# Two of eight column blocks of a gated norm on POOL instead of DVE, in a two-block transformer kernel

## The reference

```
rmsnorm(u, g) = u * rsqrt(mean(u * u) + EPS) * g

xl_new = xl + ml[2] * rmsnorm(y_l, g_post_mix[i])        # the gated norm
h2     = modulate(rmsnorm(xl_new, g_pre_mlp[i]), ml[3], ml[4])
xl_new = xl_new + ml[5] * rmsnorm(sqrelu_mlp_2(h2, ...), g_post_mlp[i])
# and the same for the context xc, with mc instead of ml, where the layer isn't the last
```

## Time and profile before

| | |
|---|---|
| median of 3 runs | 1733.2 us (1731.16 to 1733.64) |
| the profiled execution | 1732.92 us |
| its span | 1731.1 us |
| PE busy | 1624.5 us (94%) |
| DVE busy | 1155.1 us (67%) |
| ACT busy | 541.2 us (31%) |
| POOL busy | 342.6 us (20%) |

### The profile page before, as it was taken

How to read it: one execution, slowest core, us unless ns; L and a number is a source line. 1 busy time by engine, 2 the same in 40 slices (tenths; PEclk the granted TensorE clock), 3 DMA queues, 4 the chain that set the end, 5 groups by cost and what they waited for, 6 DMA issues and landing times.

```text
span 1731.1 us, 26810 instructions
## 1 busy us (share of the span) xinstructions
PE 1624.5 (94%) x10898; PEld 1420.1 (82%) x10898; DVE 1155.1 (67%) x1668; ACT 541.2 (31%) x1106; POOL 342.6 (20%) x308
## 2 busy tenths in 40 slices
PE   7998989999899999999888899999999988879997
PEld 6887789998788999988546588888888875679997
DVE  6754877777877788869764574444444778577776
ACT  4434241112333122153575440101012455641112
POOL 1100323332222333300000111111111100023331
PEclk9999999999999999999999999999999989989999
DMA  7843755556655555443101323222222241125551
GB/s 297 283 177 138 255 197 184 187 186 220 229 181 200 182 185 186 170 175 98 61 1 37 134 73 99 96 98 97 97 97 87 73 134 37 63 95 184 184 185 56
DMA packets 69939, 247.53 MB, mean 143 GB/s; under 512 B 7504, under 2 KB 10576, under 8 KB 69712
## 3 DMA queue, kind: packets, MB, share of 16 engines
q1 hardware_dynamic: 69840, 246.18, 41.7%
HBM read 245.10 MB, written 1.05 MB: 142 GB/s over the span
## 4 chain that ended last, share of the span: by engine, by line
PE 73%; DVE 14%; issue 7%; ACT 5%; DMA 1%; POOL 0%; SPq 0%; DVEq 0%; ACTq 0%; POOLq 0%
PE psum L371 20%; PE psum L373 19%; PE psum L372 19%; DVE lo_ring L334 2%; PE psum L1112 2%; PE psum L386 1%; PE psum L387 1%; PE psum L388 1%; DVE c_soft L2125 1%; ACT c_p L1914 1%; DVE r_x L1525 1%; DVE c_conf L2021 1%; DVE c_p L2133 1%; PE psum L486 1%; PE psum L1743 1%
## 5 line engine op out<-in xcount | busy, mean ns | idle before, releaser
L2289 POOL TENSOR_SCALAR hi_ring<-raw_ring 128x1024 fp32r<-128x1024 f32 x304 | 342.4, 1128 | 1366.9 <-PE psum L373 967.3
L334 DVE TENSOR_TENSOR lo_ring<-raw_ring,hi_ring 128x1024 fp32r<-128x1024 f32 x348 | 499.8, 1437 | 60.0 <-POOL hi_ring L2289 23.0
L371 PE MATMUL psum<-x_hi,hi_ring 128*128 128x256 f32 (+1 forms) x1464 | 465.0, 318 | 30.1 <-DVE lo_ring L334 13.6
L372 PE MATMUL psum<-x_lo,hi_ring 128*128 128x256 f32 (+1 forms) x1464 | 459.8, 314 | 0.0
L373 PE MATMUL psum<-x_hi,lo_ring 128*128 128x256 f32 (+1 forms) x1464 | 459.5, 314 | 0.0
L371 PEld LDWEIGHTS psum<-x_hi,hi_ring 128*128 128x128 f32 x1464 | 284.7, 194 | 53.8 <-issue 22.4
L371 PE MATMUL psum<-hid_hi,hi_ring 128*128 128x256 f32 (+1 forms) x992 | 303.3, 306 | 0.0
L373 PE MATMUL psum<-hid_hi,lo_ring 128*128 128x256 f32 (+1 forms) x992 | 302.1, 305 | 0.0
L372 PE MATMUL psum<-hid_lo,hi_ring 128*128 128x256 f32 (+1 forms) x992 | 301.2, 304 | 0.0
L372 PEld LDWEIGHTS psum<-x_lo,hi_ring 128*128 128x128 f32 x1464 | 284.8, 195 | 15.1 <-issue 0.2
L373 PEld LDWEIGHTS psum<-x_hi,lo_ring 128*128 128x128 f32 x1464 | 284.7, 194 | 15.1
(11 more groups left out here) (423 smaller groups left out, 1997.7 us busy)
## 6 DMA issues: line engine op xcount, KB each, us to landing
raw_ring<-weights SPq DMA_DIRECT2D x460, 512.0 KB, 3.3
h_const<-hyb_consts SPq DMA_DIRECT2D x1, 1088.0 KB, 11.6
x<-xT SPq DMA_DIRECT2D x1, 1024.0 KB, 5.8
x<-ctxT SPq DMA_DIRECT2D x1, 1024.0 KB, 17.0
outT<-x SPq DMA_DIRECT2D x4, 256.0 KB, 2.5
shared<-shared_consts SPq DMA_DIRECT2D x1, 398.0 KB, 13.7
par<-params SPq DMA_DIRECT2D x1, 301.5 KB, 6.4
```

Source lines behind the costliest of these rows:

```text
L334: nc.vector.tensor_tensor(lo_ring[:, s, :], raw_ring[:, UNIT_AT[u] % RAW_SLOTS, :], hi_ring[:, s, :].bitcast(F32), ALU.subtract).then_inc( ...
L371: nc.tensor.matmul(bank(u % BANKS, T), w_hi, hi[:, k, 0:T], start=(k == 0), stop=False)
L372: nc.tensor.matmul(bank(u % BANKS, T), w_hi, lo[:, k, 0:T], start=False, stop=False)
L2289: nc.gpsimd.tensor_scalar(hi_ring[:, n % SPLIT_SLOTS, :], raw_ring[:, slot, :], 1.0, 0.0, ALU.mult, ALU.add).then_inc(hi_ready, 1)
```

## The change

In layer 0's gated norm POOL takes blocks 3 and 7, product and addition, and DVE the other six. POOL's product goes to relu2 instead of normed. POOL counts a flag of its own, pool_updated, and ACT waits for this one ahead of the squares of blocks 3 and 7. DVE's additions of blocks 4 and 6 (the order of the places being 0, 1, 2, 4, 5, 6) must keep the count that ACT's other waits look for, so block 4 counts 2 (for 3 and 4) and block 6 counts 2 (for 6 and 7). POOL's piece stands ahead of its split of the MLP's unit 4, the one that waits for PE to finish the MLP's unit 0. Layer 1 isn't changed, nor are PE and SP.

```diff
     def squares_act(act, n, T, src, name, at, place=None):
         for k in range(KT):
-            act.wait_ge(flag(name), at + k + 1)
+            if T == TB and k in POOL_BLOCKS:
+                act.wait_ge(flag("pool_updated"), POOL_BLOCKS.index(k) + 1)
+            else:
+                act.wait_ge(flag(name), at + k + 1)
             nc.scalar.activation(sq[:, k, 0:T], src[:, k, 0:T], ACT.Square).then_inc(flag("norm_sq"), 1)
...
-        for c, (a, b) in enumerate(GATED[T]):
+        for c, (a, b) in enumerate([p for p in GATED[T] if T == SEQ or p[0] not in POOL_BLOCKS]):
             t = normed_chunk(c, a, b, T)
             by = rstd[:, 0:T].unsqueeze(1).broadcast_to([P, b - a, T])
             link(nc.vector.tensor_tensor(t, y[:, a:b, 0:T], by, ALU.mult))
-            nc.vector.tensor_tensor(x[:, a:b, 0:T], t, x[:, a:b, 0:T], ALU.add).then_inc(flag("x_updated"), b - a)
+            counts = COUNTED[a] if T == TB else b - a
+            nc.vector.tensor_tensor(x[:, a:b, 0:T], t, x[:, a:b, 0:T], ALU.add).then_inc(flag("x_updated"), counts)
+
+    POOL_BLOCKS = (3, 7)
+    COUNTED = {0: 1, 1: 1, 2: 1, 4: 2, 5: 1, 6: 2}
+
+    def gated_pool(pool, n):
+
+        pool.wait_ge(flag("norm_rstd"), n + 1)
+        pool.wait_ge(flag("y_scaled"), KT * ((n - 3) // 2))
+        for i, k in enumerate(POOL_BLOCKS):
+            nc.gpsimd.tensor_tensor(relu2[:, i, :], y[:, k, :], rstd[:, :], ALU.mult).then_inc(flag("pool_product"), 1)
+            pool.wait_ge(flag("pool_product"), i + 1)
+            nc.gpsimd.tensor_tensor(x[:, k, :], relu2[:, i, :], x[:, k, :], ALU.add).then_inc(flag("pool_updated"), 1)
...
             for n, u in enumerate(SPLIT_UNITS):
+                if u == U_L2MLP[0] + 4:
+                    gated_pool(pool, LAYERS[0].norm + 1)
                 if u in ACT_HI:
                     continue
```

## The result

| | before | changed |
|---|---|---|
| median of 20 runs | 1732.59 us | 1738.07 us |
| ratio | | 1.0025, 95% interval 1.0017 to 1.0032 |
| the profiled execution, its span | 1732.92, 1731.1 us | 1737.69, 1735.8 us |

The changed kernel is slower by 0.25%, 4.3 us (2.9 to 5.5); this is the distance of the means, 1737.49 and 1733.20 us, while the medians are 5.5 us apart. Two later measurements of the same code gave 1.0015 and 1.0027; all three together are about 3.9 us.

The account below looks back on a forecast made before the run. The prediction took PE waiting for DVE in layer 0's gated norm as the bound. Turns +3.12, two pairs gone -2.65 and a second tail block +0.86 gave +1.3 us on 1733.2, so 1734.5 us, range 1731.1 to 1737.9.

Parts of the forecast that it names:

- Where the kernel is bound, and that it passes on: In layer 0's gated norm PE waits for DVE; what the norm gains or loses passes one for one to the end.
- Two pairs away, -2.65: Two of DVE's eight product and addition pairs leave its chain in the gated norm, 2.65 us less.
- Turns between DVE and POOL: In the gated norm DVE operations with both inputs in SBUF alternate with POOL's four operations, +3.12 us; chance 0.57.
- rival A: DVE and POOL work side by side in the norm without hindering each other, -1.79 us, 1731.4 us; chance 0.10.
- The price of a turn: Each POOL operation between two of DVE's in the norm costs DVE 0.78 us, four of them +3.12 us.
- p: Time of one new POOL operation in the norm, taken as 1.05 us, with ends of 0.53 and 2.1 us.
- The second block in the tail, +0.86: After DVE's end PE has two blocks to add instead of one before the statistics, +0.86 us.
- Rival D, the clock: PE falls to half clock in the norm's sums, +1.7 us on top, +3.0 in all, 1736.2 us; chance 0.11.
- Rival B: POOL's two-input operations in the norm take well above 1.05 us, giving 1738.7 us at 2.1 us each; chance 0.10.
- C: POOL comes late in the norm, after DVE's queued operations or by a slow first start, 1734.9 or 1733.8 us; chance 0.12.
- C's second case: POOL's first product in the norm starts 6 us late, at 982.9; claimed +0.6 us, 1733.8 us.
- POOL's flags hold nobody: POOL finishes blocks 3 and 7 at 979.9 and 982.8, before ACT reaches them at about 984 and 988.

Follow-up runs that it names:

- e3: The changed kernel with rstd and the products for DVE in PSUM, so each DVE operation has one SBUF input; ratio 0.9985 to the kernel before.
- e2: The changed kernel without POOL's four operations, blocks 3 and 7 of the update left out; ratio 0.9988 to the kernel before.
- e4: The changed kernel with rstd and the products for DVE in PSUM and POOL on blocks 2 and 5; ratio 0.9980 to the kernel before.
- e8: The changed kernel itself, measured a second time with nothing altered; ratio 1.0015 to the kernel before.
- e6: The changed kernel with only block 3 on POOL and seven blocks on DVE; ratio 1.0003 to the kernel before.

## Why the prediction was right in its mechanism and small in its size

- **Where the kernel is bound, and that it passes on**: right. M rose by 2.82 us and PE's first MLP matmul moved from 17.32 to 20.13 us after the first product, +2.81; behind the MLP it was +2.95 (332.06 to 335.01 us). That this goes one for one to the end the traces can't show: the part behind the MLP takes 419.4 to 425.0 us, whichever the kernel.
- **Two pairs away, -2.65**: right but for 0.14 us, the two additions that count by 2 and start 0.07 us late. That edit I had costed at nothing.
- **Turns between DVE and POOL**: right, against rival A. e3 shows the condition.
- **The price of a turn**: the term that was mis-sized. I took p = 1.05 from the operation with one input of 1024 columns; two inputs of 512 take 1.28. A turn costs 1.02 instead of 0.78, four of them 4.1 instead of 3.12: 1.0 us of the error. The formula p - 0.27 holds (1.01). The estimate of 1.12 us from the Trainium skill, GPSIMD Engine Reference, section 3.1, was nearer, and too small as well. POOL going first didn't change the number of turns, four.
- **The second block in the tail, +0.86**: right in itself (e2, e3: 2.74; e3 against e4: 0.86). In the changed kernel the tail is 3.12, because of the next point.
- **Rival D, the clock**: it wasn't a rival but a part of the result, in every trace of the changed kernel (0.50 in 982 to 986). I gave it 0.11. The rows that told it were there: in layer 1 PE is busy 1.30 of 4.00 us and gets 0.60 after it. Its price in M was less than my 1.7, which was for a half clock in the tail: the clock was back at 1.00 from 986.6 us, before DVE's end, and only PE's backlog reached the tail.
- **Rival B, C**: neither. p is 1.28, under the 1.58 from which B decides, and POOL started at once. (C's second case has a slip: 988.1 + 1.88 - 989.47 is +0.5 us, not +0.6.)
- **POOL's flags hold nobody**: right. POOL ended at 982.21, ACT came to block 3 after 984.

The sum with the measured terms: 4.1 - 2.65 + 0.14 + 0.86 + 0.3 to 0.6 = 2.8 to 3.1 us of M. Forecast was +1.3 with a range of -2.1 to +4.7; measured were 4.3, 2.6 and 4.7. The range held with the ratio, 1.0025 x 1733.2 = 1737.5 us; the median itself, 1738.07, is 0.2 us past its end of 1737.9. That it held owes something to luck, since its upper end stood for p = 1.9 and not for a clock or a rest. The time fell on the side to which I gave 0.15. Of the 2.6 us between the forecast and the mean of the three, 1.0 is p, 0.14 the counts, 0.3 to 0.6 the clock in M. The remaining 1 us isn't in the norm, and what it is stays open. The scatter behind the MLP is larger than it, and in e8, where the mean granted clock was that of the kernel before (0.9771 and 0.9773), nothing of it is left: 2.6 us measured, 2.8 in M.

## What to carry to other kernels

Work that moves to POOL cost DVE nothing where DVE, meanwhile, read at most one operand from SBUF (e3, e4); otherwise each POOL operation went onto DVE's chain nearly whole, 1.02 of its 1.28 us, and DVE would have done the same in 0.66. Put a shared factor and the intermediate product in PSUM, and let the engine on the critical path have the last block: that turned +0.25, +0.15 and +0.27% into -0.20 and -0.14%. When a producer slows down, look at what its consumer's clock does while it waits. And before explaining 1 or 2 us of a time, compare the granted clocks of the executions in a part that the edit doesn't touch.

## What the runs showed of the hardware that I hadn't expected

- A tensor_tensor of 128x512 fp32 on POOL takes 1.27 to 1.29 us undisturbed, a tensor_scalar of 128x1024 1.05.
- POOL's profiled 1.59 to 1.71 us in the changed kernel are waiting and work together; its first operation there (1.28) and e3 show the work.
- A DVE instruction that reads and writes PSUM at 128x512 costs the same 0.69 us as one in SBUF, so the move to PSUM was free (e3 and e2: DVE's part 8.20 us in both).
- A DVE operation that raises a semaphore by 2 instead of 1 started 0.07 us later behind its own predecessor (0.79 for 0.72 us), in the changed kernel, e2 to e6, and in layer 1 before. It follows the count to whichever pair has it; why is open.
- Between executions of the same code, the part behind the MLP took up to 5.5 us more or less (419.40 and 424.86 us in two traces of the changed kernel), in step with the granted clock (0.97 and 0.95).
